# Two modulation vectors moved from TensorE products to GpSimd sums

## What is computed

```python
c_act = jax.nn.silu(c); c_ctx_act = jax.nn.silu(c_ctx)
mx = jnp.split((c_act @ w_mod[l] + b_mod[l])[:, None, :], N_MOD, axis=-1)
mc = jnp.split((c_ctx_act @ w_mod[l] + b_mod[l])[None, None, :], N_MOD, axis=-1)
x = x + 0.5 * mx[2] * swiglu_2(modulate(rms_norm(x), mx[0], mx[1]), *ffn1)
```

## Time and profile before

| | |
|---|---|
| median of 3 runs (lowest to highest) | 2552.76 us (2552.27 to 2554.6) |
| the profiled execution | 2556.66 us |
| its span, first to last instruction | 2554.9 us |
| mean granted clock of TensorE | 0.985 of full |
| TensorE busy | 2453.7 us, 96% |
| VectorE busy | 1620.8 us, 63% |
| ScalarE busy | 1035.0 us, 41% |
| GpSimd busy | 0.2 us, 4 instructions |

### The profile page before, as it was taken

How to read it: one execution, slowest core, us unless ns; L and a number is a source line. 1 busy time by engine, 2 the same in 40 slices (tenths; PEclk the granted TensorE clock), 3 DMA queues, 4 the chain that set the end, 5 groups by cost and what they waited for, 6 DMA issues and landing times. The chain is left out here.

```text
span 2554.9 us, 36957 instructions
## 1 busy us (share of the span) xinstructions
PE 2453.7 (96%) x15134; PEld 2136.2 (84%) x15134; DVE 1620.8 (63%) x2674; ACT 1035.0 (41%) x1676; POOL 0.2 (0%) x4
## 2 busy tenths in 40 slices
PE   7999899899999999998889999999999998988999
PEld 6998799899978888886668888888888887878999
DVE  6768544756576777568768776638555537846553
ACT  5545544445332222265544222214222226744442
POOL 0000000000000000000000000000000000000000
PEclk9999999999999999999989999999999999999999
DMA  8644543455645555354014555424555426502654
GB/s 277 204 150 133 172 124 99 149 182 159 183 157 165 173 171 165 106 166 139 1 33 132 174 166 167 145 97 155 173 165 168 133 90 178 186 9 67 183 183 147
DMA packets 143658, 372.28 MB, mean 146 GB/s; under 512 B 22378, under 2 KB 40450, under 8 KB 143490
## 3 DMA queue, kind: packets, MB, share of 16 engines
q1 hardware_dynamic: 143202, 369.60, 46.7%
q10 hardware_dynamic: 288, 0.31, 0.1%
HBM read 368.71 MB, written 1.15 MB: 145 GB/s over the span
## 5 line engine op out<-in xcount | busy, mean ns | idle before, releaser
L357 PE MATMUL psum<-normed_hi,weights_hi 128*128 128x256 f32 (+2 forms) x2664 | 886.6, 333 | 29.0 <-DVE normed_lo L636 9.0
L357 PE MATMUL psum<-normed_lo,weights_hi 128*128 128x256 f32 (+2 forms) x2664 | 870.3, 327 | 0.0
L357 PE MATMUL psum<-normed_hi,weights_lo 128*128 128x256 f32 (+2 forms) x2664 | 869.2, 326 | 0.0
L305 DVE TENSOR_TENSOR weights_lo<-weights_raw,weights_hi 128x1024 fp32r<-128x1024 f32 (+2 forms) x547 | 657.7, 1211 | 255.9 <-ACT weights_hi L299 253.4
L299 ACT CAST weights_hi<-weights_raw 128x1024 fp32r<-128x1024 f32 (+2 forms) x547 | 562.8, 1036 | 318.7 <-DMA weights_raw<-in_w_down 199.9
L357 PEld LDWEIGHTS psum<-normed_hi,weights_hi 128*128 128x128 f32 (+1 forms) x2664 | 511.3, 192 | 91.5 <-issue 35.7
L357 PEld LDWEIGHTS psum<-normed_hi,weights_lo 128*128 128x128 f32 (+1 forms) x2664 | 512.5, 192 | 41.4
L357 PEld LDWEIGHTS psum<-normed_lo,weights_hi 128*128 128x128 f32 (+1 forms) x2664 | 512.5, 192 | 39.8 <-issue 1.2
L951 DVE SCALAR_TENSOR_TENSOR arena<-arena,cond 128x512 f32<-128x512 f32 x392 | 273.1, 747 | 6.9 <-DMA arena<-in_w_mod 2.9
L357 PE MATMUL psum<-hidden_hi,weights_hi 128*128 128x512 f32 (+1 forms) x594 | 219.4, 369 | 0.0
L357 PE MATMUL psum<-hidden_lo,weights_hi 128*128 128x512 f32 (+1 forms) x594 | 217.4, 366 | 0.0
(11 more groups left out here) (273 smaller groups left out, 2792.8 us busy)
## 6 DMA issues: line engine op xcount, KB each, us to landing
weights_raw<-in_w_gu SPq DMA_DIRECT2D x220, 512.0 KB, 3.6
arena<-in_w_mod SPq DMA_DIRECT2D x256, 256.0 KB, 3.0
weights_raw<-in_w_down SPq DMA_DIRECT2D x110, 512.0 KB, 3.6
weights_raw<-in_w_x SPq DMA_DIRECT2D x24, 512.0 KB, 5.8
weights_raw<-in_w_qk SPq DMA_DIRECT2D x24, 512.0 KB, 3.6
weights_raw<-in_w_z SPq DMA_DIRECT2D x16, 512.0 KB, 3.6
weights_raw<-in_w_g SPq DMA_DIRECT2D x16, 512.0 KB, 3.6
weights_raw<-in_w_ssm_branch SPq DMA_DIRECT2D x16, 512.0 KB, 3.6
```

Of the source, the lines that this page charges most:

```text
L305: ve.tensor_tensor(w_lo[:, c % RING, a], w_raw[:, c % RING, a], w_hi[:, c % RING, a].bitcast(F32), ALU.subtract).then_inc(lo_ready, 1)
L357: last = te.matmul(out, a, b, start=start and n == 0, stop=stop and n == 2)
```

## The change

The class `Modulation` goes, and the first two vectors are made by `ModulationSums` too, in 4 rounds of half a vector. In this first use (`pool=True`) the multiplications and additions run on GpSimd, not on VectorE. GpSimd has no fused form here: for each half chunk and side it runs one multiplication (`tensor_scalar`) into a product tile and one addition (`tensor_tensor`) into the sum; the first half chunk of a round needs only the multiplication. So a round is 16 multiplications and 14 additions of 128 x 512, the whole 64 and 56. TensorE keeps the 8 matmuls of `pick` and one transpose for each round.

The sums, products and the ring of three half chunks lie in parts of `normed_raw` and `resid` that the first segment leaves free. The track now has 48 steps between 0.1 and 0.95 of the segment. A round is 12 steps: eight in which SP asks for the half chunk three ahead (which waits until the half chunk three before it has been added on both sides), two empty ones (FIRST_LATE), one in which TensorE waits for the finished sums and adds the partitions and ScalarE copies the rows, and one in which TensorE turns them and VectorE adds the bias. By the order that `woven` gives, the first round starts behind conv3, and its partition sums stand behind conv17; those of the other rounds stand behind z10, qk11 and v5.

`cond` shrinks from 32 to 2 columns and needs no zeroing. The semaphore `half_added` is split into one for each side, so a wait for both sides is two waits; this holds for the later vectors as well, whose order and arithmetic stay.

```diff
-MOD_W = 2 * P
-MOD_CHUNK = 4 * MOD_W
-MOD_ROUNDS = NMOD * D // MOD_CHUNK
-MOD_RING = 6
-MOD_FIRST = 2
-HALF_W = MOD_CHUNK // 2
+MOD_CHUNK = D
+HALF_W = D // 2
 HALF_RING = 3
+FIRST_VECTORS, FIRST_LATE = 2, 2
...
-        cond = sb("cond", KD, 32)
+        cond = sb("cond", KD, 2)
...
-        half_added, half_summed, half_rows, half_turned, half_read = (
-            sem("mod_half_" + n) for n in ("added", "summed", "rows_copied", "rows_turned", "columns_read"))
+        half_added = [sem(f"mod_half_side_{side}_added") for side in range(2)]
+        half_products, half_summed, half_rows, half_turned, half_read = (
+            sem("mod_half_" + n) for n in ("products_ready", "summed", "rows_copied", "rows_turned", "columns_read"))
...
-                act.wait_ge(cond_zero, 1)
...
-                ve.memset(cond[:], 0.0).then_inc(cond_zero, 1)
...
-        class Modulation(Stage):
...
+        class SumSpace:
+            def __init__(self, sums, ring, rows, products=None):
+                self.sums, self.ring, self.rows, self.products = sums, ring, rows, products
+        first_space = SumSpace([normed_raw[:, k:k + 2, CTX] for k in (0, 2)],
+                               [resid[:, k:k + 2, CTX] for k in (0, 2, 4)], at(25600, 2, P),
+                               [normed_raw[:, k:k + 2, CTX] for k in (4, 6)])
+        later_space = SumSpace([at(22528 + HALF_W * side, 2, S) for side in range(2)],
+                               [at(23552 + HALF_W * s, 2, S) for s in range(HALF_RING)],
+                               small[:, 256:256 + 2 * P].rearrange("p (b n) -> p b n", b=2))
         class ModulationSums(Stage):
-            def __init__(self, vectors, after=()):
-                self.after = after
+            def __init__(self, vectors, space=later_space, after=(), late=0, pool=False):
+                self.after, self.space, self.late, self.pool = after, space, late, pool
                 self.halves = [(layer, which, half) for layer, which in vectors for half in range(2)]
                 self.round0 = take("half_rounds", len(self.halves))
                 self.chunk0 = take("half_chunks", KD * len(self.halves))
-                self.added = []
-                for layer, which, _ in self.halves:
-                    each = len(self.sides(layer, which))
-                    self.added.append((take("half_adds", KD * each), each))
-                self.n = (KD + 2) * len(self.halves)
+                self.added = [{side: take(f"half_adds_{side}", KD) for side in self.sides(layer, which)}
+                              for layer, which, _ in self.halves]
+                self.n = (KD + 2 + late) * len(self.halves)
             def sides(self, layer, which):
                 return (0, 1) if layer == 0 or which < 5 else (0,)
-            def added_by(self, m):
-                first, each = self.added[m // KD]
-                return half_added, first + (m % KD + 1) * each
+            def at(self, i):
+                r, j = divmod(i, KD + 2 + self.late)
+                return r, j if j < KD else j - self.late if j >= KD + self.late else -1
+            def wait_added(self, engine, m):
+                for side, first in self.added[m // KD].items():
+                    engine.wait_ge(half_added[side], first + m % KD + 1)
             def load(self, sp, m):
                 if m < KD * len(self.halves):
                     c, (layer, which, half) = self.chunk0 + m, self.halves[m // KD]
                     if m >= HALF_RING:
-                        sp.wait_ge(*self.added_by(m - HALF_RING))
-                    sp.dma_start(half_ring[c % HALF_RING], W["w_mod"][(layer * NMOD + which) * KD + m % KD]
-                                 [:, half * HALF_W:(half + 1) * HALF_W]).then_inc(half_landed[c % HALF_RING], 16)
+                        self.wait_added(sp, m - HALF_RING)
+                    sp.dma_start(self.space.ring[c % HALF_RING], W["w_mod"][(layer * NMOD + which) * KD + m % KD]
+                                 [:, half * HALF_W:(half + 1) * HALF_W].rearrange("p (a n) -> p a n", a=2)
+                                 ).then_inc(half_landed[c % HALF_RING], 16)
             def sync(self, sp, i):
-                r, j = divmod(i, KD + 2)
+                r, j = self.at(i)
                 if i == 0:
                     for event in self.after:
                         sp.wait_ge(*event)
                     for m in range(HALF_RING):
                         self.load(sp, m)
-                if j < KD:
+                if 0 <= j < KD:
                     self.load(sp, r * KD + j + HALF_RING)
+            def start(self, engine, r, j, side):
+                c, nth, first = self.chunk0 + r * KD + j, self.round0 + r, self.added[r][side]
+                engine.wait_ge(half_landed[c % HALF_RING], 16 * (c // HALF_RING + 1))
+                if j == 0 and nth >= 1:
+                    engine.wait_ge(half_summed, nth)
+                if j > 0:
+                    engine.wait_ge(half_added[side], first + j)
+                return self.space.sums[side], self.space.ring[c % HALF_RING], cond[:, j, side:side + 1]
+            def gpsimd(self, pool, i):
+                r, j = self.at(i)
+                if not self.pool or not 0 <= j < KD:
+                    return
+                if i == 0:
+                    pool.wait_ge(cond_in, 1)
+                for side in self.added[r]:
+                    total, weights, scalar = self.start(pool, r, j, side)
+                    if j == 0:
+                        ge.tensor_scalar(total, weights, scalar, None, ALU.mult).then_inc(half_added[side], 1)
+                    else:
+                        ge.tensor_scalar(self.space.products[side], weights, scalar, None, ALU.mult
+                                         ).then_inc(half_products, 1)
+                if j > 0:
+                    for side in self.added[r]:
+                        total = self.space.sums[side]
+                        pool.wait_ge(half_products, 2 * ((KD - 1) * r + j - 1) + side + 1)
+                        ge.tensor_tensor(total, total, self.space.products[side], ALU.add
+                                         ).then_inc(half_added[side], 1)
             def tensor(self, pe, i):
-                r, j = divmod(i, KD + 2)
+                r, j = self.at(i)
                 nth = self.round0 + r
                 if j == KD:
                     sides = self.sides(*self.halves[r][:2])
-                    pe.wait_ge(*self.added_by(r * KD + KD - 1))
+                    self.wait_added(pe, r * KD + KD - 1)
                     if nth >= 1:
                         pe.wait_ge(half_read, nth)
                     for side in sides:
                         for g in range(4):
                             last = te.matmul(psum[32 * g:32 * g + 32, MOD_BANK, 0:P], pick[:, side, :],
-                                             half_sums[:, side, g * P:(g + 1) * P], start=side == 0,
-                                             stop=side == sides[-1], tile_position=(0, 32 * g))
+                                             self.space.sums[side][:, g // 2, g % 2 * P:(g % 2 + 1) * P],
+                                             start=side == 0, stop=side == sides[-1], tile_position=(0, 32 * g))
                     last.then_inc(half_summed, 1)
                 if j == KD + 1:
+                    pe.wait_ge(const_in, 32)
                     pe.wait_ge(half_rows, nth + 1)
-                    te.transpose(psum[:, MOD_BANK, 2 * P:3 * P], half_rows_sb[:, nth % 2, :], ident
+                    te.transpose(psum[:, MOD_BANK, 2 * P:3 * P], self.space.rows[:, nth % 2, :], ident
                                  ).then_inc(half_turned, 1)
...
                 if j == KD + 1:
...
-                if j < KD:
+                if 0 <= j < KD and not self.pool:
...
-                sp.wait_ge(mod_read, MOD_FIRST)
+                sp.wait_ge(half_read, 2 * FIRST_VECTORS)
...
-        mod_ring0 = [t[:, k:k + 4, CTX] for t in (resid, normed_raw, under_hi) for k in (0, 4)]
+        first_sums = ModulationSums([(0, which) for which in range(FIRST_VECTORS)], first_space, [(cond_in, 1)],
+                                    late=FIRST_LATE, pool=True)
...
-            ([Modulation(MOD_FIRST, mod_ring0)], 0.1, 0.38),
+            ([first_sums], 0.1, 0.95),
...
+        @block.gpsimd
+        def _(pool):
+            for steps in plan:
+                for stage, i in steps:
+                    stage.gpsimd(pool, i)
```

109 lines of the change are left out of this document (18 added, 91 removed).

## The result

The changed kernel took 2578.43 us (median; 2575.75 to 2581.87) against 2553.07 of the kernel before on the same chip: 1.0098 times as long, 95% interval 1.0086 to 1.0111. So 25.4 us slower, where the forecast was 9.0 faster and the range ended at 2561. The profiled execution took 2578.01 us (span 2575.8), 21.35 more than that of before (which lay 3.9 above its median).

A forecast was written before the change was run, and what follows sets the result against it. TensorE, busy 96% of the span, was taken as the bound. 12.99 us saved less 3.52 of new TensorE work and 0.5 of waits gave 9.0 us less, a median of 2543.8; forecast's own range 2541 to 2547.6, widened to 2561.

The forecast's parts named there:

- T: GpSimd's time for one half chunk, two multiplications and two additions of 128 x 512: taken as 4.2 us, bounds 2.46 and 8.2.
- the deadline of 4.95: Longest T, in us, with the first round's sums ready by conv17's end at 73.27; each us above costs 7 us.
- a rival: GpSimd and VectorE keep each other out: first sums 11.6 us late, scan 3 more; 7.1 us slower, 2559.9; chance 0.20.
- What goes: On TensorE, four steps of four products, with the weight wait, two pairs of transposes and the clock fall: 12.99 us less.
- What comes on TensorE: Four rounds of 8 small matmuls and one transpose, all on the path: 3.52 us more.
- T, first term: GpSimd's multiplication of 128 x 512, taken as 1.7 times VectorE's 0.482 us, the ratio from a one-column memset.
- What is queued behind: Weight loads behind SP's waits for GpSimd, held 5 to 7 us each: 8.4 us of delay covered, 7.0 used, hidden.
- My signs: Success: no TensorE idle time before L919, the first round's sums. Late sums: L919 released by GpSimd, SP waiting over 8 us.
- Behind conv: Later rounds' sums have room up to T = 7.7 us; VectorE's lengthening in the scan costs 3 us, only in a rival.
- The row copies: ScalarE's row copies for the two halves, four instead of two with VectorE's bias steps: short and in the cover.
- The clock: TensorE's clock fall near 50 us, behind the wait for `w_mod` weights, does not recur if nothing new waits: 1.49 us less.
- M1's wait: TensorE's wait for `w_mod` weights in the first four-product step, 2.41 us before one group; that step booked at 5.18 us.

The follow-up runs named there:

- e14_spread_later: Changed kernel with GpSimd's rounds spread over segment 1 and the next stretch, GpSimd idle at segment 1's end; 2545.42 us, ratio 0.9966 to the kernel before.
- e3_ring8: Changed kernel with eight slots for half chunks instead of three, loads in the same steps; 2572.64 us, ratio 1.0081 to the kernel before.
- e1_probe: Separate kernel looping GpSimd operations alone and beside VectorE or ScalarE: multiplication 1.562 us alone; addition 1.262 alone, 2.137 beside a subtraction of two SBUF operands.
- e7_one_source: Changed kernel with VectorE's splits of the first 80 weight chunks reading one SBUF operand, low part left out; 2562.67 us, ratio 1.0036 to the kernel before.
- e8_fitted: Changed kernel with eight slots, two-input multiplication (tensor_tensor), rounds placed by GpSimd's pace and last row copy late; 2568.26 us, ratio 1.0055 to the kernel before.
- e5_late_copy: e2_one_side with the last round's partition sums, row copy and transposition behind v_proj's eighth step; 2547.91 us, ratio 0.9974 to the kernel before.
- e2_one_side: Changed kernel with only the token side's sums on GpSimd, the context side's left out; 2552.53 us, ratio 1.000 to the kernel before.
- e15_after_late_copy: Changed kernel, both sides, with the last round's partition sums, row copy and transposition moved as in e5_late_copy; 2575.97 us, ratio 1.0087 to the kernel before.
- e6_cheap: Changed kernel with GpSimd multiplying by tensor_tensor and a repeated column instead of tensor_scalar; 2579.81 us, ratio 1.0105 to the kernel before.

## Why the prediction was wrong, step by step

Two steps failed. The time of a half chunk, T, was put at 4.2 us and measured 6.7, over the deadline of 4.95 that the prediction itself had worked out. And behind conv, VectorE's lengthening was put at 3 us, in a rival alone, where VectorE was short of time. What the change takes off TensorE, and what it puts on, came out.

**What goes: right.** By conv23 I booked 5.18 + 5.88 + 0.22 + 1.49 = 12.8 us. e14_spread_later, which has no partition sums before that, is 12.5 ahead there, and conv17 was read at 73.89 where I had put its end at 73.27.

**What comes on TensorE: right.** With four rounds of 0.88 and 0.5 for waits I had 9.0 us; e14_spread_later has 10.8 at the gates, 10.0 when all four rounds are done, and its median is 8.1 under before. The forecast's 2543.8 comes near that kernel, not this one.

**T, first term: the multiplication was mis-sized.** I carried one ratio, that of a memset of a single column, over to it: 0.82 us, and 1.56 was measured (T alone 5.65). With 16 multiplications and 14 additions the first round takes 42.7 us, so the sums would be ready at 38.2 + 42.7 = 80.9, 7.6 late. This step alone takes T over the deadline of 4.95.

**T, second term: contention, which I gave 0.20 as a rival, is real.** The first round took 53.3 us, 10.6 more; in all it was 18.2 late, which e3_ring8 shows as one wait. The rival had 16.9 for its share, from a full block in each chunk; the probe shows the two engines lengthening each other, but less than that. So its direction was right, its mechanism too strong, and its total too cheap as it stood on my T. e1_probe shows the contention by itself and e7_one_source in place.

**What is queued behind: named, and then set to nothing.** "hidden, with little to spare: it breaks near the same T as the sums do" was right. With T = 6.7 SyncE was held 82.6 us, and TensorE came to the sums so late that it waited there only 2.9. My signs, "no idle time before L919" and "SP waiting for GpSimd over 8 us", saw next to nothing of a kernel 10 us late at conv23: the wait was 2.9 and SyncE's longest 7.6.

**Behind conv: not priced.** I held that the other rounds have room up to T = 7.7, and it is true of the sums, which were in time. But I gave VectorE's own lengthening 3 us. The changed kernel loses 7.5 us from conv23 to qk23, and e8_fitted, where no sum is ever late, 17.7: there it is the largest failed step. VectorE has two operands in SBUF in its splits and in the scan's products, and idled 27 us before its splits there; that was its cover, and I didn't work it out.

**The row copies: costed at "short, and in that cover".** Their duration is 0.25 us; their wait for TensorE in v_proj, with casts behind it, costs 4.6 to 6.6 by the times of e5_late_copy against e2_one_side, and some 3 in the changed kernel (e15_after_late_copy). I had looked at their length and at conv alone, and not at what each queue does at the new place.

**The clock: right where I looked.** Without M1's wait the low clock near 50 us was gone, and with it the 1.49; but TensorE's new waits in conv brought others: from 50 to 100 us, in stretches of ten, the granted clock was 0.88, 0.95, 0.66, 1.00 and 0.83 in the changed kernel and 1.00 throughout in e14_spread_later. Up to the sums it shows as 38 start-to-start distances longer than 0.12, 3.5 us together. These lie in time that GpSimd's lateness takes anyway, since TensorE still came 2.9 us too early for the sums; behind them it is 1.1 us more.

Of the 34.3 us between the lead of 12.5 that was to be had and the 21.8 lost at the gates, conv holds 22.8, z_proj and qk_proj 7.5, v_proj and the copy 4. In conv, 18.2 are the first round's lateness: 7.6 the multiplication's own price and the rest contention. Then come the round's own matmuls (some 0.9, which e14_spread_later does not have in conv) and 3.5 that TensorE's timeline shows behind them, 2.4 in three waits behind the late weights and 1.1 by the clock. The division of the 18.2 is worked out from the probe, and not shown by a run: e6_cheap, which was to show it, lost behind conv what it won there.
